# Differential attention: queries and keys turned through VectorE and DRAM, scores in rounded passes

## The reference

```python
h = rms_norm(x, norm_g)                       # (512, 1024)
z = h @ w_in                                  # (512, 9216), split into ten parts
o_r = retention(q_r, k_r, v_r); y_r = (rms_norm(o_r) * silu(gate_r)) @ ret_w_o
qd = rms_norm(q_d.reshape(S, 8, 2, 64), diff_q_norm_g)      # 8 heads, 2 maps, 64 features
kd = rms_norm(k_d.reshape(S, 8, 2, 64), diff_k_norm_g)
s[h, j] = (qd[:, h, j] / 8) @ kd[:, h, j].T - slope[h] * distance   # causal, j = 0, 1
a[h] = softmax(s[h, 0]) - lam * softmax(s[h, 1])
o_d = rms_norm(a[h] @ v_d[:, h])              # then gate, diff_w_o -> y_d
x = x + (sigmoid(mg_r) * y_r + sigmoid(mg_d) * y_d) @ w_out
```

## Time and profile before

| what | before |
|---|---|
| median of three runs | 909.25 us |
| profiled execution | 909.13 us |
| its span, first to last instruction | 907.3 us |
| granted TensorE clock | 1.00 (2.4 GHz) |
| PE, the projections' 512-column passes | starts 0.23 us apart |
| HBM, mean over the span | 89 GB/s |

### The profile page before, as it was taken

The page is one execution under the profiler, slowest core; times in us unless marked ns, Lnnn a source line. Parts: engine busy times, 40 slices in busy tenths (PEclk is TensorE's granted clock), DMA queues, the critical chain, the costliest instruction groups (busy, mean ns, idle before and its releaser), DMA issues.

```text
span 907.3 us, 12615 instructions
## 1 busy us (share of the span) xinstructions
PE 895.9 (99%) x4648; PEld 712.8 (79%) x4648; DVE 422.9 (47%) x957; ACT 397.2 (44%) x872; POOL 439.7 (48%) x376
## 2 busy tenths in 40 slices
PE   8999999999999999999999999999999998999998
PEld 6878888888888877777777788889888765777776
DVE  4211251545114413467474455646648866553631
ACT  5533323334223344454554444244435774655531
POOL 5544436445446654646444344545448382234362
PEclk9999999999999999999999999999999999999999
DMA  8532222313333322122212234233433321011113
GB/s 305 163 96 82 69 70 73 107 58 113 94 97 101 104 81 83 48 70 70 70 50 68 70 112 143 93 106 97 119 102 105 94 85 55 25 47 47 47 48 116
DMA packets 43564, 81.29 MB, mean 90 GB/s; under 512 B 4416, under 2 KB 6208, under 8 KB 43504
## 3 DMA queue, kind: packets, MB, share of 16 engines
q1 hardware_dynamic: 42016, 79.95, 29.1%
q10 hardware_dynamic: 1488, 0.55, 0.2%
HBM read 78.36 MB, written 2.12 MB: 89 GB/s over the span
## 4 chain that ended last, share of the span: by engine, by line
PE 84%; DVE 8%; issue 3%; POOL 2%; DMA 2%; ACT 1%; SPq 0%; ACTq 0%; DVEq 0%; POOLq 0%
PE Z L1706 23%; PE Z L1708 22%; PE Z L1707 22%; PE A L1883 3%; PE A L1806 2%; PE A L1921 2%; PE A L1892 2%; PE A L1818 2%; DVE z_sb L1237 1%; POOL w_lo L941 1%; PE A L1866 1%; DMA raw<-in_w_in 1%; DVE rstd L1140 1%; PE A L1831 1%; PE A L1716 1%
## 5 line engine op out<-in xcount | busy, mean ns | idle before, releaser
L941 POOL TENSOR_TENSOR w_lo<-raw,w_hi 128x512 fp32r<-128x512 f32 (+1 forms) x262 | 346.0, 1327 | 443.8 <-ACT w_hi L574 443.1
L574 ACT CAST w_hi<-raw 128x512 fp32r<-128x512 f32 (+1 forms) x262 | 157.9, 614 | 294.8 <-PE Z L1708 261.7
L1706 PE MATMUL Z<-w_hi,hT_hi 128*128 128x512 f32 (+1 forms) x544 | 218.1, 401 | 0.0
L1708 PE MATMUL Z<-w_hi,hT_lo 128*128 128x512 f32 (+1 forms) x544 | 211.5, 389 | 0.0
L1707 PE MATMUL Z<-w_lo,hT_hi 128*128 128x512 f32 (+1 forms) x544 | 210.9, 388 | 0.0
L1706 PEld LDWEIGHTS Z<-w_hi,hT_hi 128*128 128x128 f32 x544 | 102.4, 188 | 27.5 <-issue 8.3
L1708 PEld LDWEIGHTS Z<-w_hi,hT_lo 128*128 128x128 f32 x544 | 102.1, 188 | 20.8
L1707 PEld LDWEIGHTS Z<-w_lo,hT_hi 128*128 128x128 f32 x544 | 102.5, 188 | 17.6
L1706 PE MATMUL Z<-hT_hi,w_hi 128*128 128x512 f32 x260 | 113.2, 435 | 1.0 <-POOL w_lo L941 1.0
L1708 PE MATMUL Z<-hT_hi,w_lo 128*128 128x512 f32 x260 | 102.1, 393 | 0.0
L1707 PE MATMUL Z<-hT_lo,w_hi 128*128 128x512 f32 x260 | 101.6, 391 | 0.0
(11 more groups left out here) (239 smaller groups left out, 1298.4 us busy)
## 6 DMA issues: line engine op xcount, KB each, us to landing
raw<-in_w_in SPq DMA_DIRECT2D x91, 512.0 KB, 3.7
raw<-in_w_out SPq DMA_DIRECT2D x16, 512.0 KB, 3.6
raw<-in_ret_w_o SPq DMA_DIRECT2D x8, 512.0 KB, 3.3
raw<-in_diff_w_o SPq DMA_DIRECT2D x8, 512.0 KB, 3.3
x_sb<-in_x SPq DMA_DIRECT2D x4, 512.0 KB, 5.8
x_sb<-in_xT SPq DMA_DIRECT2D x4, 512.0 KB, 6.8
out<-x_sb SPq DMA_DIRECT2D x8, 256.0 KB, 3.2
raw<-in_w_in SPq DMA_DIRECT2D x4, 416.0 KB, 3.4
```

The source lines that it names most:

```text
L574: act.copy(w_hi[:, s % SPLIT_SLOTS, 0:width], raw[:, c % RAW_SLOTS, s - CHUNK_START[c], 0:width]).then_inc(hi_ready, 1)
L941: pool.tensor_tensor(w_lo[:, s % SPLIT_SLOTS, 0:width], raw[:, c % RAW_SLOTS, s - CHUNK_START[c], 0:width], w_hi[:, s % SPLIT_SLOTS, 0:wid ...
L1706: pe.matmul(out, l_hi, r_hi, start=first, stop=False)
L1708: return pe.matmul(out, l_lo, r_hi, start=False, stop=last)
```

## The change: what it does

Queries and keys are no longer transposed by TensorE. After a group's normalisation VectorE transposes each 128 columns in 32x32 squares (`dve.transpose`, four instructions of 128x512 per group), SyncE's queue writes the squares to DRAM so that they stand transposed there (four DMAs of 64 KB per head's 128 columns, in runs of 32 elements, 128 bytes), and reads each map back twice, into rows 0 to 63 and 64 to 127 (two DMAs of 256 KB for a head's queries, two for its keys). ScalarE rounds the queries with both gains (`queries_high`) and VectorE replaces rows 64 to 127 by the low half (`queries_low`); ScalarE rounds the keys (`keys_high`), POOL subtracts (`keys_low`). A map's scores are then two rounded passes over 128 rows: (high and low queries) times high keys, and times low keys. The step for the turn goes, 72 steps are left of 86, and they are spread otherwise: the first comes at slot 19 instead of 12, 30 of them before slot 140 and 42 from there to 208. `ROWS_OUT`, `QUERIES_IN` and `KEYS_IN` say before which slab's weights SyncE issues each write and read. POOL's squares of groups 10 and 11 are taken two and two, and the first half's output normalisation (`norms["first"]`) moves from slabs 37 and 38 to 40 and 41.

```diff
-DIFF_FIRST, DIFF_SECOND, DIFF_THIRD, DIFF_LAST = 10, 116, 160, 208
+DIFF_FIRST, DIFF_SECOND, DIFF_LAST = 15, 140, 208
+DIFF_STEPS = 2 * (4 * H + 4)
...
     if v < DIFF_SECOND:
-        return 36 * (v - DIFF_FIRST + 1) // (DIFF_SECOND - DIFF_FIRST)
-    if v < DIFF_THIRD:
-        return 36 + 22 * (v - DIFF_SECOND + 1) // (DIFF_THIRD - DIFF_SECOND)
-    return min(86, 58 + 28 * (v - DIFF_THIRD + 1) // (DIFF_LAST - DIFF_THIRD))
+        return 30 * (v - DIFF_FIRST + 1) // (DIFF_SECOND - DIFF_FIRST)
+    return min(DIFF_STEPS, 30 + (DIFF_STEPS - 30) * (v - DIFF_SECOND + 1) // (DIFF_LAST - DIFF_SECOND))
...
+ROWS_OUT = ((-4, -2, 0, 0), (2, 4, 12, 14), (26, 28, 30, 32), (34, 36, 38, 40))
+QUERIES_IN = (4, 8, 14, 22, 30, 38, 42, 46)
+KEYS_IN = (6, 10, 16, 24, 36, 40, 44, 46)
...
+            def rows_written(i, w):
+
+                v = qk_dram[:, :, :]
+                sp.wait_ge(rows_ready, 4 * i + w + 1)
+                for q in range(4):
+                    to = bass.AP(tensor=v.tensor, offset=(4 * i + w) * P * S + 32 * q,
+                                 ap=[[S, 32], [P, TT], [32 * S, 4], [1, 32]])
+                    sp.dma_start(to, sgd_sb[32 * q:32 * (q + 1), w, :].rearrange("r (t n c) -> r t n c", t=TT, c=32)
+                                 ).then_inc(rows_out[w], 16)
+
+            def turned_twice(i, w, j):
+                v = qk_dram[:, :, :]
+                return bass.AP(tensor=v.tensor, offset=(4 * i + w) * P * S + DK * S * j, ap=[[0, 2], [S, DK], [1, S]])
+
+            def queries_read(h):
+
+                half, w = divmod(h, 4)
+                sp.wait_ge(rows_out[w], 64 * (2 * half + 1))
+                if h:
+                    sp.wait_ge(q_lo, 2 * h)
+                for j in range(2):
+                    sp.dma_start(q_raw[:, j, :], turned_twice(2 * half, w, j)).then_inc(q_in, 16)
+
+            def keys_read(h):
+
+                half, w = divmod(h, 4)
+                sp.wait_ge(rows_out[w], 64 * (2 * half + 2))
+                if h >= 2:
+                    sp.wait_ge(s_mm, 8 * (h - 1))
+                for j in range(2):
+                    sp.dma_start(k_raw(h, j), turned_twice(2 * half + 1, w, j)).then_inc(k_in[h % 2], 16)
...
+            def queries_high(h):
+
+                act.wait_ge(q_in, 32 * (h + 1))
+                if h >= 2:
+                    act.wait_ge(s_mm, 8 * (h - 1))
+                for j in range(2):
+                    act.activation(q_both[:, diff_slot_of(h, j), :], q_raw[:, j, :], ACT.Copy,
+                                   scale=cols[:, 35:36]).then_inc(q_hi, 1)
+
+            def keys_high(h):
+
+                act.wait_ge(k_in[h % 2], 32 * (h // 2 + 1))
+                for j in range(2):
+                    act.copy(k_high[:, diff_slot_of(h, j), :], k_raw(h, j)).then_inc(k_hi, 1)
...
-                    if i in (1, 2) and h + 1 < H:
-                        (diff_queries if i == 1 else diff_keys)(h + 1)
-                        yield
+                    if i == 1 and h + 1 < H:
+                        queries_high(h + 1)
+                    yield
+                    if i == 1 and h + 1 < H:
+                        keys_high(h + 1)
...
+            def keys_low(h):
+
+                for j in range(2):
+                    pool.wait_ge(k_hi, 2 * h + j + 1)
+                    slot = diff_slot_of(h, j)
+                    pool.tensor_tensor(k_low[:, slot, :], k_raw(h, j), k_high[:, slot, :], ALU.subtract).then_inc(k_lo, 1)
...
+                    if g and g - 1 in HEAD_NORM and g < G_LAYER2 and k < 5:
+
+                        for t in (2 * k - 6, 2 * k - 5):
+                            c0 = HEAD_NORM[g - 1]
+                            pool.wait_ge(z_by_act, act_evacs[g - 1] + t + 1)
+                            square(z_sb[:, t, c0:c0 + 512], 512, squares_1)
...
+                for w in range(4 if rows is not None else 0):
+                    yield
+                    dve.wait_ge(head_normed, TT * (rows + 1))
+                    if rows:
+                        dve.wait_ge(rows_out[w], 64 * rows)
+                    dve.transpose(sgd_sb[:, w, :], z_sb[:, :, c0 + P * w:c0 + P * (w + 1)]).then_inc(rows_ready, 1)
                 yield
...
+                    if i == 2 and h + 1 < H:
+                        queries_low(h + 1)
...
+            def queries_low(h):
+
+                low = slice(DK, P)
+                for j in range(2):
+                    dve.wait_ge(q_hi, 2 * h + j + 1)
+                    q = q_both[low, diff_slot_of(h, j), :]
+                    dve.scalar_tensor_tensor(q, q_raw[low, j, :], cols[low, 35:36], q, ALU.mult, ALU.subtract).then_inc(q_lo, 1)
...
-                    if g == G_DIFF0 + 4 and k in (5, 6):
+                    if g == G_DIFF0 + 5 and k in (0, 1):
                         next(norms["first"])
...
-                    pe.wait_ge(qk_out, 2 * h + 2)
+                    pe.wait_ge(q_lo, 2 * h + 2)
+                    pe.wait_ge(k_lo, 2 * h + 2)
...
-                            rows = slice(DK * j, DK * (j + 1))
-                            pe.matmul(A[j][:, score_columns(i, True)], qT[rows, h % 2, P * i:P * (i + 1)],
-                                      kT[rows, h % 2, 0:P * (i + 1)], start=True, stop=True).then_inc(s_mm, 1)
+                            slot, bank = diff_slot_of(h, j), A[j][:, score_columns(i, True)]
+                            q = q_both[:, slot, P * i:P * (i + 1)]
+                            pe.matmul(bank, q, k_high[:, slot, 0:P * (i + 1)], start=True, stop=False)
+                            pe.matmul(bank, q, k_low[:, slot, 0:P * (i + 1)], start=False, stop=True).then_inc(s_mm, 1)
...
-                    if i in (1, 2) and h + 1 < H:
-                        diff_turn(h + 1, i - 1)
-                        yield
```

More of the change, by code:

```diff
@@ L271, in build @@
         m_sb = sb("m_sb", [P, TT, D], F32)
+        with ExitStack() as scope:
+            sb("d_rows", [P, 4, S], F32R, scope)
+            k_low = sb("k_low", [P, 4, S], F32R, scope)
         sgd_sb = sb("sgd_sb", [P, KD, S], F32)
@@ L275, in build @@
                           for v in (m_sb, x_sb, o_sb))
+        with ExitStack() as scope:
+            q_both = sb("q_both", [P, 4, S], F32R, scope)
+            k_high = sb("k_high", [P, 4, S], F32R, scope)
         qT = sb("qT", [P, 4, S], F32)
@@ L354, in build @@
         r_xe, q_latent = sem("r_xe"), sem("q_latent")
-        qk_t, qk_out, bias_r = sem("qk_t"), sem("qk_out"), sem("bias_r")
+        rows_ready, bias_r = sem("rows_ready"), sem("bias_r")
+        rows_out = [sem(f"rows_out{w}") for w in range(4)]
+        q_in, k_in = sem("q_in"), [sem("k_in0"), sem("k_in1")]
+        q_hi, q_lo, k_hi, k_lo = sem("q_hi"), sem("q_lo"), sem("k_hi"), sem("k_lo")
         s_mm, s_max, s_exp, s_comb = sem("s_mm"), sem("s_max"), sem("s_exp"), sem("s_comb")
@@ L525, in _ @@
                     sp.wait_ge(row_out, 16)
+                for i in range(4):
+                    for w in range(4):
+                        if SLAB0[g] + k - SLAB0[G_DIFF0] == ROWS_OUT[i][w]:
+                            rows_written(i, w)
+                for h in range(H):
+                    if SLAB0[g] + k - SLAB0[G_DIFF0] == QUERIES_IN[h]:
+                        queries_read(h)
+                    if SLAB0[g] + k - SLAB0[G_DIFF0] == KEYS_IN[h]:
+                        keys_read(h)
                 if g == G_DIFF_OUT + 1 and k == 0:
@@ L831, in diff_slot @@
                 if g == G_DIFF0 and k == 1:
-                    diff_queries(0)
-                    diff_keys(0)
+                    queries_high(0)
+                if g == G_DIFF0 and k == 3:
+                    keys_high(0)
                 if g + 1 in TURNED and k >= 4:
@@ L1084, in diff_slot @@
                     diff_bias(0)
+                if g == G_DIFF0 and k == 3:
+                    keys_low(0)
                 for half in range(2):
@@ L1110, in _ @@
                     retention(SLAB0[g] + k - 3)
[L1111 removed]
+                    if g and g - 1 in HEAD_NORM and g >= G_LAYER2 and k < 7:
                         c0, t = HEAD_NORM[g - 1], k - 3
                         pool.wait_ge(z_by_act, act_evacs[g - 1] + t + 1)
[L1115 removed]
+                        square(z_sb[:, t, c0:c0 + 512], 512, squares_2)
+                    if g and g - 1 in HEAD_NORM and g < G_LAYER2 and k < 5:
[3 more added lines that the diff above has]
+                            square(z_sb[:, t, c0:c0 + 512], 512, squares_1)
         @block.vector
@@ L1238, in head_scale, with head_norm @@
                                       ALU.mult).then_inc(head_normed, 1)
+                for w in range(4 if rows is not None else 0):
[4 more added lines that the diff above has]
+                    dve.transpose(sgd_sb[:, w, :], z_sb[:, :, c0 + P * w:c0 + P * (w + 1)]).then_inc(rows_ready, 1)
                 yield
-            def head_norm(c0, squares, turns):
+            def head_norm(c0, squares, turns, rows):
                 for t in range(TT):
```

(11 more changed lines are left out.)

43 lines of the change are left out of this document (17 added, 26 removed).

## The result

| | median us | range, runs | against before |
|---|---|---|---|
| before | 909.26 | 909.01 to 909.88 (4) | |
| changed | 1033.1 | 1031.5 to 1034.2 (3) | 1.1359 [1.1343, 1.1375] |
| changed, with the experiments | 1030.5 | 1029.2 to 1030.9 (4) | 1.1330 [1.1313, 1.1347] |

The forecast was 902.4 us, the range 894.5 to 913. The changed kernel is 124 us slower than before. Two executions are in no median here: one of the changed kernel, 1314.95 us at a mean granted clock of 0.65 where its others had 0.94 to 0.95, and one of ten of `e15_norm_later_narrow`, 2237.6 us, whose cause is open.

What follows compares the result with a forecast made beforehand. TensorE, busy 99% of the span, was taken as the bound. A gross gain of 14.2 us less waits of 4, 2 and 1.5 left 6.7: 909.13 - 6.7 = 902.4 us, range 894.5 to 913.

Steps and rivals of the forecast that it cites:

- Turns and scores: On TensorE: removing 64 transposes gains 7.2 us, scores as two rounded passes gain 6.1 us.
- Rival D: Rounded score passes of 128 and 256 columns cost as much as 512: 6.9 us more, 909.3, no change; chance 0.06.
- At 2 us each from 319 on they land at about 328.5: At the start, on SyncE's queue: landing of query read, weights and key read, 512 KB each, before the first scores.
- these waits hide: Later heads' reads and waits on SyncE's queue are covered by weights split early; without cover each late head costs 2.7 us.
- B: Rival: narrow 128-byte writes keep SyncE's queue long; gain gone at 4.1 us a block, 917 at 8; chance 0.13.
- The narrow writes: On SyncE's queue: each 128-row block's packets keep the queue 0.75 us beyond their issue, counted twice in the start's wait.
- The start: TensorE reaches the first scores at 330.5 and waits 4 us for low keys, at 333 plus the writes' delay.
- Beside TensorE: Added work: VectorE's 16 transposes and 16 low halves at 0.69 us each, 22 us; POOL's 16 subtractions at 1.3.
- All three have room over the whole stage; two places don't: VectorE, ScalarE and POOL fit except at the start (4 us) and in the dense steps (2 and 1.5 us).
- Rival C: VectorE becomes the bound in the dense steps, 0.5 us a block for 17 blocks: 907.4, or 911; chance 0.13.

Runs made afterwards that it cites:

- e15_norm_later_narrow: The norm later kernel with the low halves of queries and keys taken of 8 of 512 columns (scores without correction): 912.0 us, 1.0022 of before.
- e7_one_turn: The kernel before with one of the four transposes of each turn instead of four, 48 of 64 left out: 905.45 us, 0.9959.
- later reads: The kernel with reads of 64 rows, with the later heads' query and key reads moved back on SyncE's queue: 936.2 us.
- both halves narrow: The later reads kernel with the low halves of keys and queries taken of 8 of 512 columns, second score pass on high halves: 920.7 us.
- norm later: Changed kernel with reads of 64 rows, later reads, writes where rows are ready, first score block and second half's squares, sums, normalisation 4 slots later: 926.5 us.
- e14_pauses: The kernel before, with four pauses of TensorE in the same stage while POOL fills an unused tile, nothing else of the change: 931.6 us.
- e2_reads_64: The changed kernel with each read of turned rows as two DMAs of 64 rows, one per half of the partitions: 938.5 us, 1.0315 of before.
- e13_rows_128: The changed kernel with each read taking the block's 128 rows once instead of 64 rows twice (scores of wrong values): 934.5 us.
- e8_keys_narrow: The later reads kernel with the keys' low halves taken of 8 of 512 columns, second score pass on high halves: 924.6 us.

## Why the prediction was wrong

**The account.** From each trace: TensorE's pauses between 300 and 640 us (two matmuls starting over 0.75 us apart, less 0.23), the length of stretches at 1.2 GHz there, and the remainder: span less 907.3, plus 11.9 us for what the change gains on TensorE (5.3 for the turns by `e7_one_turn`, 6.6 for the scores), less the pauses beyond the 2.0 of before.

| kernel | span | pauses | at 1.2 GHz | remainder |
|---|---|---|---|---|
| changed | 1027.1 | 24: 104.4 | 99.0 | 29.3 |
| reads of 64 rows | 938.0 | 17: 31.5 | 27.3 | 13.2 |
| later reads | 935.1 | 16: 29.0 | 30.7 | 12.7 |
| both halves narrow | 917.4 | 11: 19.9 | 6.8 | 4.2 |
| norm later | 923.8 | 9: 21.5 | 20.5 | 8.8 |

The remainder is 0.4 to 0.6 of the time at 1.2 GHz (in the changed kernel less, as much of that time TensorE stood still anyway). In `e14_pauses`, where nothing is gained, the same sum leaves 7.8 us for 17.1 at 1.2 GHz. With 7.2 us for the turns, as their gaps have it, each remainder is 1.9 larger: 0.48 to 0.55 of that time in three kernels, 0.9 in the one with both halves narrow, where it is 6.1 for 6.8. So pauses and clock account for the loss but for some 2 or 3 us.

**Turns and scores: right.** The turns' gaps are as I priced them (7.2 us), though leaving out 48 of the 64 transposes gave 4.0 us and not 5.4, for the new waits. A block of 512 now costs 0.90 us (384.14 to 385.04 in the kernel with reads of 64 rows), where the prediction had 0.92:

```profile
384.14 0.39 PE L1899 MATMUL A<-k_high,q_both 128*128 128x512 f32 x1
384.36 0.39 PE L1900 MATMUL A<-k_low,q_both 128*128 128x512 f32 x1
384.59 0.39 PE L1899 MATMUL A<-k_high,q_both 128*128 128x512 f32 x1
384.82 0.39 PE L1900 MATMUL A<-k_low,q_both 128*128 128x512 f32 x1
385.04 0.39 PE L1808 MATMUL Z<-w_hi,hT_hi 128*128 128x512 f32 x1
```

By the same reading 384 columns cost 0.71, against 0.70, and 128 with 256 gain 0.12, against 0.07: 8 x (0.36 + 0.34 + 0.12) = 6.6 us, against 6.1. Rival D is out. Together that is 11.9 us by the experiment, 13.8 by the gaps, not counting the wait of 0.9.

**The failed step: "At 2 us each from 319 on they land at about 328.5".** I gave the query read and the key read, 512 KB each, the time of a 512 KB load of weights. Each is two DMAs of 256 KB at 51 GB/s: 10.3 us instead of 2. I counted the reads' bytes and packets and never looked at how their descriptors spread over the engines, though the access pattern is in the diff. The same step carried the later heads ("these waits hide"): the waits on the queue do hide, but the transfers behind them did not. Mended, it is worth 92 us in `e2_reads_64` and 96 in `e13_rows_128`. None of the rivals had it; B had the right queue with the wrong transfer. Mending it would not have saved the forecast: 938.5 is still above its range, for the two terms below, the work beside TensorE and the price of a pause.

**The narrow writes: right.** 0.9 us in all at the reads' mended speed, where I had 1.5, and 3.1 in the changed kernel, both hardly above the spread. In the changed kernel they land in the time of a load:

```profile
L517 SPq DMA_DIRECT2D qk_dram<-sgd_sb x64: 569/630/3336, 293.9 to 525.2; - x64
...
DMA to landing us min/median/max: 2.1/3.4/6.9
```

Only the issue was dearer than my 0.47: 0.63 us. The 9.8 us row was no neighbour for these packets, as argued.

**The start: near, once the reads are mended.** With reads of 64 rows TensorE starts the first scores at 336.2 after a wait of 3.5 us for the low keys, where I had 4, from 330.5 on. In the changed kernel it was 9.1.

**Beside TensorE: wrong in size.** VectorE's transposes took 0.67 us as forecast (0.69), but a low half of queries 1.41 (median; I had 0.69) and one of keys 1.74 on POOL (I had 1.3):

```profile
L1538 DVE SCALAR_TENSOR_TENSOR q_both<-q_raw,cols,q_both x16: 752/1415/1790, 329.0 to 521.8; 64x512 fp32r<-64x512 f32 x16
```

```profile
L1084 POOL TENSOR_TENSOR k_low<-sgd_sb,k_high x16: 1254/1742/1842, 333.6 to 523.0; 128x512 fp32r<-128x512 f32 x16
```

They stand at the same step of a head and run side by side. With POOL's subtraction of 8 columns (`e8_keys_narrow`) the queries' takes 0.75 at the median, close to the forecast, against 1.56 in the kernel that it was made from; so it is POOL's work beside it that doubles it, and I had priced each engine alone:

```profile
L1538 DVE SCALAR_TENSOR_TENSOR q_both<-q_raw,cols,q_both x16: 747/753/1418, 328.7 to 505.1; 64x512 fp32r<-64x512 f32 x16
```

"All three have room over the whole stage; two places don't" missed a third place, the two normalisations of the second half amid heads 2 and 3. I allowed 3.5 us for VectorE; the low halves alone cost 15. Rival C saw VectorE as the bound in the dense steps. It is 68% busy there in the best kernel (65.0 of 95 us), so not full on the average; whether its holes or POOL's order hold TensorE up in those steps no run here separates, as narrowing POOL's work shortens VectorE's too.

**Missing altogether: the price of a pause.** I added waits at their length. A wait of 3 to 5 us costs TensorE about half as much again, on the average, in slow passes after it: 22.2 us for 15.2 in `e14_pauses`. In the kernel with reads of 64 rows that is 13 us, more than the whole gain.

**Left open.** Where the last 2.6 us of `e15_norm_later_narrow` lie. Whether low halves on an engine that has nothing behind them would be cheaper: every version here keeps them on POOL and VectorE. No version of the change tried here beats the kernel before.

## What to carry to other kernels

Read a DMA's access pattern before its size. Here a broadcast of 2 written first made a 256 KB read take 5 us and held up the loads behind it on the queue; with 64 or 128 outermost that was gone. A stretch in which all compute engines idle and the DMA share is a round 2/16 was that fault's sign. When TensorE is 99% busy, price a wait of some microseconds at one and a half times its length (22.2 us for 15.2 here). And price an operation that is added to a half-empty engine with what runs beside it and what stands behind it: here it took twice its time beside POOL's, and moving it half a block gained nothing.

## What the runs showed of the hardware

- While DMAs ran whose source's outermost dimension is 2, the DMA share was 0.13, that of 2 of 16 engines, at 51 GB/s; the next issue on the same queue then took up to 7.0 us on SyncE, instead of 0.37. With 64 outermost the share was 0.91 to 0.95.
- 65,536 bytes written to DRAM in 512 packets of 128 bytes land in 3.4 us (median) and cost 0.63 us of issue.
- Four pauses of TensorE of 2.8 to 5.0 us each brought the granted clock to 1.2 GHz in a kernel that otherwise held 2.4 GHz; passes of 512 columns then start 0.43 us apart instead of 0.23. In other kernels of this case one of 3.6 us did not.
- Rounded matmuls of 128 rows by 512 columns on the stacked halves start 0.23 us apart, as the projections' do.
- POOL's subtraction lengthens a VectorE operation on SBUF tiles that runs beside it: 1.56 us at the median, 0.75 with POOL's of 8 columns. POOL's own was 1.25 at the least and 1.74 at the median.
